# Attention scores on TensorE: fp32 products on 64 partitions each, or split fp32r operands stacked on 128 partitions and always 256 columns wide

## The reference

```python
def neighbourhood_attention(q, k, v, rpb):
    b, t, h, dh = q.shape
    rows = t // GRID_W
    kh = min(NA_KH, rows)
    qg = q.reshape(b, rows, GRID_W, h, dh) * (dh ** -0.5)
    ...
    def one_row(r):
        ...
        s = jnp.einsum('bqhd,bjkhd->bhqjk', qr, kb).astype(jnp.float32)
        ...
        s = jnp.where(col_in[:, None, :], s + bias[None], -jnp.inf)
        p = jax.nn.softmax(s.reshape(b, h, GRID_W, kh * GRID_W), axis=-1)
        p = p.reshape(b, h, GRID_W, kh, GRID_W).astype(vb.dtype)
        return jnp.einsum('bhqjk,bjkhd->bqhd', p, vb)
```

## Time and profile before

| | |
|---|---|
| runs | 2142.4, 2145.27, 2147.19 us (median 2145.27) |
| span of the profiled execution | 2143.2 us |
| own device time of the profiled execution | not listed apart; the median of the runs is 2.1 us above its span |
| PE matmuls busy | 2099.4 us, 98% of the span, at full granted clock |
| DVE, ACT, POOL busy | 51%, 37%, 43% |
| DMA | 86 GB/s in the mean |
| layer 1's 16 steps | from about 1373 us of the span, with the output tail to 2143 us |

### The profile page before, as it was taken

How to read it: one execution, slowest core, us unless ns; L and a number is a source line. 1 busy time by engine, 2 the same in 40 slices (tenths; PEclk the granted TensorE clock), 3 DMA queues, 4 the chain that set the end, 5 groups by cost and what they waited for, 6 DMA issues and landing times.

```text
span 2143.2 us, 31195 instructions
## 1 busy us (share of the span) xinstructions
PE 2099.4 (98%) x12580; PEld 1789.7 (84%) x12580; DVE 1089.1 (51%) x1866; ACT 800.1 (37%) x1943; POOL 924.6 (43%) x623
## 2 busy tenths in 40 slices
PE   8999999999999999999999999999999999999997
PEld 7888887788898888787788887888888888888885
DVE  4104332598898898897712233144333423541447
ACT  4123122465464555473322111143424323432343
POOL 5533332333343343325742332654454445544544
PEclk9999999999999999999999999999999999999999
DMA  5221112335232233235331111322131223123213
GB/s 189 90 68 53 51 50 74 137 98 143 80 109 80 70 118 100 78 119 173 125 125 50 50 50 50 96 87 68 59 88 59 68 59 96 40 68 86 69 50 118
DMA packets 206685, 184.19 MB, mean 86 GB/s; under 512 B 23916, under 2 KB 172684, under 8 KB 206541
## 3 DMA queue, kind: packets, MB, share of 16 engines
q1 hardware_dynamic: 206541, 182.20, 27.7%
HBM read 168.19 MB, written 12.21 MB: 84 GB/s over the span
## 4 chain that ended last, share of the span: by engine, by line
PE 50%; DVE 4%; issue 1%; ACT 0%; DMA 0%; POOL 0%; DVEq 0%; POOLq 0%; ACTq 0%
PE bank L214 25%; PE bank L264 9%; PE bank L574 6%; PE bank L2411 2%; PE bank L2439 2%; PE bank L1067 2%; PE bank L2422 2%; PE bank L1093 1%; DVE acc L944 1%; PE bank L1131 1%; DVE acc L940 1%; DMA R<-macc_dram 0%; PE bank L447 0%; DVE R L422 0%; PE bank L2483 0%
## 5 line engine op out<-in xcount | busy, mean ns | idle before, releaser
L188 POOL TENSOR_SCALAR Wh<-Wraw 128x1024 fp32r<-128x1024 f32 x217 | 245.9, 1133 | 1100.2 <-issue 755.2
L214 PE MATMUL bank<-Hh,Wh 128*128 128x512 f32 (+1 forms) x1936 | 664.6, 343 | 3.2 <-ACT R L817 1.4
L214 PE MATMUL bank<-Hl,Wh 128*128 128x512 f32 (+1 forms) x1936 | 652.0, 337 | 0.0
L214 PE MATMUL bank<-Hh,Wl 128*128 128x512 f32 (+1 forms) x1936 | 651.0, 336 | 0.0
L191 POOL TENSOR_TENSOR Wl<-Wraw,Wh 128x1024 fp32r<-128x1024 f32 x217 | 550.6, 2537 | 18.1
L214 PEld LDWEIGHTS bank<-Hh,Wh 128*128 128x128 f32 x1936 | 367.7, 190 | 51.0 <-issue 10.8
L214 PEld LDWEIGHTS bank<-Hh,Wl 128*128 128x128 f32 x1936 | 367.3, 190 | 39.0
L214 PEld LDWEIGHTS bank<-Hl,Wh 128*128 128x128 f32 x1936 | 367.9, 190 | 36.6 <-issue 1.7
L298 DVE TENSOR_TENSOR acc<-bank,acc 128x512 f32<-128x512 f32 x240 | 165.0, 690 | 166.3 <-PE bank L264 165.5
L264 PE MATMUL bank<-Wh,Mh 128*128 128x512 f32 x528 | 208.7, 395 | 8.7 <-DVE acc L298 7.6
L264 PE MATMUL bank<-Wh,Ml 128*128 128x512 f32 x528 | 205.7, 390 | 0.0
(11 more groups left out here) (259 smaller groups left out, 3124.0 us busy)
## 6 DMA issues: line engine op xcount, KB each, us to landing
Wraw<-in_na_w_in_dram SPq DMA_DIRECT2D x80, 512.0 KB, 3.8
Wraw<-in_ssd_w_in_dram SPq DMA_DIRECT2D x57, 512.0 KB, 4.2
Wraw<-in_w_out_dram SPq DMA_DIRECT2D x48, 512.0 KB, 3.3
R<-acs_dram SPq DMA_DIRECT2D x16, 1536.0 KB, 6.8
Wraw<-in_w_mem_kv_dram SPq DMA_DIRECT2D x32, 512.0 KB, 3.9
R<-gs_dram SPq DMA_DIRECT2D x32, 128.0 KB, 3.5
R<-R SPq DMA_DIRECT2D x32, 128.0 KB, 3.6
macc_dram<-acc SPq DMA_DIRECT2D x1, 3072.0 KB, 11.5
```

The source lines that it names most:

```text
L188: pool.tensor_scalar(Wh[:, s, :], Wraw[:, s, :], 1.0, 1.0, ALU.mult, ALU.mult).then_inc(pool_c, 1)
L214: mm = pe.matmul(DB[h.k % 2][:, 0:t1 - t0], w[:, k, :], x[:, k, t0:t1], start=(k == 0 and i == 0), stop=(k == KC - 1 and i == 2))
```

## The change

The scores are no longer plain fp32 matmuls. The change makes three stacked tensors for each pair of heads, and does two fp32r matmuls over all 128 partitions where there was one fp32 matmul over 64:

- `Qs` (Q_split): for head h, its own 64 rows hold the high part of q, the other 64 rows hold its low part.
- `Kh` (K_high): for head h, the high part of k on both halves of the partitions.
- `Kl` (K_low, and for head 1 M_last_low): the low part of k on the head's own rows, zero on the others.
- `Qs` times `Kh` gives high x high + low x high; `Qs` times `Kl` gives high x low. Both are added in PSUM.
- Every block is computed 256 columns wide, at column 0 or 256 of its bank (`wide`); DVE reads the same 256, 192 or 160 columns as before, and the second blocks of banks 1 and 2 have moved to columns 320 and 256.
- ACT writes the high parts (`split_q`, `split_k`, two copies of 64 x 768 each) and the second copy of the high part of k (`repeat_k`, two more). DVE makes the low parts (`low_parts`, four subtractions of 64 x 768, and once two fills with zeros).
- PE waits for `k_twice` and `qk_low` before the scores.
- `Q_split` and `K_high` lie where `gain` and a part of the residual were kept, so SP loads those two behind the last scores instead of in step 1.

```diff
@@ class Places
                 self.mix = tensor_at("M_last", 0, [P, 3, T], F32R)
+                self.q_split = tensor_at("Q_split", 12096, [P, 2, T], F32R)
+                self.k_high = tensor_at("K_high", 13632, [P, 2, T], F32R)
+                self.k_low = tensor_at("K_low", 10224, [P, T], F32R)
@@ attention_phase
+            Qs, Kh, Kl = place.q_split, place.k_high, [place.k_low[:, :], place.mix_low[:, :]]
+            ROWS_OF = [slice(0, 64), slice(64, P)]
             B = [(0, 0, 256, NP_ + 128, NP_ + 64, 0, 3), (0, 256, 256, NP_ + 256, NP_ + 192, 0, 4),
-                 (1, 0, 192, NP_, NP_, 256, 2), (1, 192, 192, NP_ + 384, NP_ + 320, 448, 5),
-                 (2, 0, 160, 0, 0, 640, 0), (2, 160, 160, 128, 96, 800, 1)]
+                 (1, 0, 192, NP_, NP_, 256, 2), (1, 320, 192, NP_ + 384, NP_ + 320, 448, 5),
+                 (2, 0, 160, 0, 0, 640, 0), (2, 256, 160, 128, 96, 800, 1)]
+            def wide(c0, k0):
+                c = c0 // 256 * 256
+                return slice(c, c + 256), slice(k0 - (c0 - c), k0 - (c0 - c) + 256)
@@ sync
-                    if n == 1:
-                        sp.wait_ge(begun.mixed, 12)
-                        sp.wait_ge(begun.x1_stored, 16)
-                        sp.dma_start(gain, post_g[1:2, :].broadcast_to([P, D])).then_inc(gain_landed, 16)
-                        load_res(sp, 2)
...
                 def end():
                     load_out(sp, 1, slice(14 * P, 16 * P))
+                    sp.wait_ge(begun.x1_stored, 16)
+                    sp.wait_ge(scored, 2 * PAIRS)
+                    sp.dma_start(gain, post_g[1:2, :].broadcast_to([P, D])).then_inc(gain_landed, 16)
+                    load_res(sp, 2)
@@ scalar
+                def split_q(n):
+                    act.wait_ge(dense_free, HF["act"].value + 2)
+                    for h, f in enumerate(ROWS_OF):
+                        i = act.activation(Qs[f, h, :], qF[f, :], ACT.Copy)
+                    i.then_inc(qk_high, 1)
+                def split_k(n):
+                    act.wait_ge(dense_free, HF["act"].value + 2)
+                    for h, f in enumerate(ROWS_OF):
+                        i = act.activation(Kh[f, h, :], kF[f, :], ACT.Copy)
+                    i.then_inc(qk_high, 1)
+                def repeat_k(n):
+                    for h, f in enumerate(ROWS_OF):
+                        i = act.activation(Kh[ROWS_OF[1 - h], h, :], kF[f, :], ACT.Copy)
+                    i.then_inc(k_twice, 1)
@@ scalar, step
                         probs(n - 1, 1)
+                    split_q(n)
                     if n == LAST:
                         act_take(act, [lambda b: act.activation(kF[:, 0:NP_], b[:, 0:NP_], ACT.Copy),
                                        lambda b: act.activation(kF[:, NP_:T], b[:, 0:NS], ACT.Copy)],
                                  between=lambda: take_pt(n - 1, (0,)))
+                        split_k(n)
+                        repeat_k(n)
                         take_pt(n - 1, (1,))
                     else:
                         take_spans(act, kF)
+                        split_k(n)
                         if out_after(n):
                             out_units()
                         if prev:
                             take_pt(n - 1)
+                        repeat_k(n)
@@ vector
+                def low_parts(n):
+                    if n == 0:
+                        for h in range(2):
+                            c.add(dve.memset(Kl[h][ROWS_OF[1 - h], :].bitcast(F32), 0.0))
+                    dve.wait_ge(qk_high, 2 * n + 1)
+                    for h, f in enumerate(ROWS_OF):
+                        dve.tensor_tensor(Qs[ROWS_OF[1 - h], h, :], qF[f, :], Qs[f, h, :].bitcast(F32), ALU.subtract)
+                    dve.wait_ge(qk_high, 2 * n + 2)
+                    for h, f in enumerate(ROWS_OF):
+                        i = dve.tensor_tensor(Kl[h][f, :], kF[f, :], Kh[f, h, :].bitcast(F32), ALU.subtract)
+                    i.then_inc(qk_low, 1)
                 def step(n, a, prev):
+                    low_parts(n)
@@ tensor, score
+                    pe.wait_ge(k_twice, n + 1)
+                    pe.wait_ge(qk_low, n + 1)
...
+                        at, of = wide(c0, k0)
                         for h in range(2):
-                            f = slice(64 * h, 64 * h + 64)
-                            mm = pe.matmul(A[3 * h + bk][:, c0:c0 + w], qF[f, q0:q0 + P], kF[f, k0:k0 + w],
-                                           start=True, stop=True)
+                            pe.matmul(A[3 * h + bk][:, at], Qs[:, h, q0:q0 + P], Kh[:, h, of],
+                                      start=True, stop=False)
+                            mm = pe.matmul(A[3 * h + bk][:, at], Qs[:, h, q0:q0 + P], Kl[h][:, of],
+                                           start=False, stop=True)
```

More of the change, by code:

```diff
@@ L2041, in attention_phase @@
             gain_landed, prompt_gated = sem("n_gain_landed"), sem("n_prompt_gated")
+            qk_high, k_twice, qk_low = (sem("n_" + x) for x in ("qk_high", "k_twice", "qk_low"))
             bias_landed = [sem("n_bias_landed0"), sem("n_bias_landed1")]
```

## The result

The changed kernel took 2149.17 us in the median of 12 executions (2148.53 to 2152.42), the kernel before 2145.68 us (2142.4 to 2148.66, 12 executions). The ratio is 1.0021, 95% interval 1.0013 to 1.0029, which is 4.5 us more (2.8 to 6.2) of 2145.68; the two medians by themselves lie 3.5 us apart. The forecast was 2150.3 us, a ratio of 1.0023 to the median that it started from.

The account below looks back on a forecast made before the run. PE, busy 98% of the span, was taken as the bound, except at the softmax path in the last step. Terms 1.3 + 1.6 + 2.1 = 5.0 us, added to the median, gave 2150.3 us (+0.23%), range 2145.5 to 2153.5.

Parts of the forecast that it names:

- Middle steps: Scores on PE in 11 middle steps: +0.11 us each, 1.3 us in all, bounds 0 to 2.4 us.
- Steps 0, 4, 8, 12: Scores without apply_v right before them and nothing to wait for: +0.41 us, four times, 1.6 us; upper bound 2.4 us.
- the padding of 160 and 192 columns: Score blocks of 160 and 192 columns paid as 256, a third more columns, given as reason for +0.41 us.
- ACT and DVE hidden: Added ACT copies hidden behind PE's z unit with about 1 us spare; DVE's subtractions, 3.8 us a step, cost zero.
- Gain: SP's later load of gain lands about 4.2 us after issue, hidden with 7 us of cover before ACT reads it.
- The last step: Step 15: apply_v(14) waits 2.0 us for take_pt behind four ACT copies, scores end 0.1 us later; +2.1 us.
- the three terms: Middle steps 1.3 us, steps 0, 4, 8, 12 1.6 us, last step 2.1 us: 5.0 us more.
- rival 2: The wait in step 15 is absent or much shorter through quicker copies: +2.9 to 4 us, about 2148.5 us; chance 0.18.
- The faster stream (1): New score matmuls come closer together than 0.119 us; at 0.109, +1.2 us, 2146.5 us; chance 0.15.
- The upper bound of 2.5 us for the last step: Step 15 if copies don't overlap at all (4 x 0.88): a wait of 2.4 us; 2.5 us in rival 3's sum.
- More waits (3): ACT's spare microsecond in middle steps is missing, or waits and shape changes cost upper bounds: 7.3 us, 2152.6 us; chance 0.15.
- The much cheaper scores (4): Scores get much cheaper because half of the passes go; PE would save over 0.5 us a step; chance 0.04.

Follow-up runs that it names:

- g1: Kernel before, with apply_v doing the two prompt blocks first under their own semaphore so DVE gates the prompt earlier; 2138.73 us, ratio 0.9977.
- g3: e1's kernel with apply_v doing the two prompt blocks first and DVE gating the prompt earlier; 2150.26 us in one execution.
- e3: Changed kernel with each score block computed at its own width (256, 192 or 160 columns) instead of always 256; 2149.86 us, ratio 1.0019.
- e5: Kernel before with the score loops swapped: all six blocks of head 0, then all six of head 1; 2162.44 us in one execution.
- e4: Changed kernel with all its copies, subtractions, waits and moved loads, but the scores again as fp32 matmuls on 64 partitions; 2147.93 us in one execution.
- e1: Changed kernel with the four copies of step 15 (split_k, repeat_k) moved behind take_pt; 2147.12 us, ratio 1.0011 to before.
- f8: The changed kernel run once more as it is, to see what of its profile repeats; 2149.22 us.
- f7: e1's kernel with the low product on each head's own 64 partitions, blocks in four groups; 2161.17 us, ratio 1.0071 to before.
- f6: e1's kernel with the low product on each head's own 64 partitions, block by block; 2173.26 us, ratio 1.0131 to before.
- f2: Changed kernel with only repeat_k of step 15 moved behind take_pt, split_k staying in front; 3004.66 us.

## Why the prediction was right

**Middle steps: right in size and in its reason.** 0.10 us a step for 0.11 (11 of them are 1.2 us, and not the 1.3 of the sum). The stream runs at 0.118 us (0.119 forecast), the first interval behind `apply_v` is the slow one (0.224 us for 0.223) and the change to L214 isn't. g1 and g3 confirm that the loss of 0.54 us is set off by 0.44 of vanished waits.

**Steps 0, 4, 8, 12: right.** 0.37 and 0.38 us for 0.41. That these cost more than the middle ones is because nothing waited there before. The reason in the text, the padding of 160 and 192 columns, is refuted by e3: full width costs 0.1 us of it. The columns grow by 26% there (1536 against 1216), not by a third. With own widths the scores still take 2.73 us there, where the old ones take 2.26, and that is the lost sharing (e5): 24 starts one after the other instead of 12 pairs.

**ACT and DVE hidden: right.** ACT's timeline in step 4, beside the earlier trace rows:

```profile
1539.99 0.38 ACT L245 ACTIVATE R<-bank 128x256 f32<-128x256 f32 x1
1540.94 0.60 ACT L246 ACTIVATE R<-bank 128x512 f32<-128x512 f32 x1 [0.56 <-PE bank L214]
```

The cover is 0.56 us where 1 was forecast, and e4 shows that it is enough: 32.90 us with all the copies. DVE is hidden too, but its price was too low: it is busy for 100 us more, 6.2 us a step where the sum had 3.8. The subtractions of 64 x 768 in step 4, and beside them what POOL does meanwhile:

```profile
1532.78 2.72 DVE L2375 TENSOR_TENSOR K_low<-R,K_high 64x768 fp32r<-64x768 f32 x1 [0.36 <-ACT K_high L2226]
1535.51 0.95 DVE L2375 TENSOR_TENSOR M_last_low<-R,K_high 64x768 fp32r<-64x768 f32 x1
```

```profile
1531.70 2.98 POOL L191 TENSOR_TENSOR Wl<-Wraw,Wh 128x1024 fp32r<-128x1024 f32 x1
```

The first one runs against POOL's splitting of a weight unit for 1.90 us and takes 2.72, the second, of the same shape, has POOL idle and takes 0.95. It is so for all of them in the traces of after and of e1: none that had POOL idle took over 0.96 us. In step 15 the low part of k is ready at 2079.56 for it, where the sum had 2078.8, still ahead of `apply_v`.

**Gain: right.** SP issues it at 2097.45 and ACT reads it at 2108.84; it lands in about 4.2 us.

**The last step: the mechanism right, the term too small.** The wait is 2.15 us for 2.0. The step that was off is "copies back to back start about 0.1 us before the previous one ends". ACT's timeline in step 15:

```profile
2074.08 0.60 ACT L2251 ACTIVATE R<-bank 128x512 f32<-128x512 f32 x1 [2.23 <-PE bank L214]
2074.71 1.70 ACT L2226 ACTIVATE K_high<-R 64x768 fp32r<-64x768 f32 x2
2076.44 1.70 ACT L2231 ACTIVATE K_high<-R 64x768 fp32r<-64x768 f32 x2
2078.05 0.57 ACT L2211 ACTIVATE R<-bank 128x512 f32<-128x512 f32 x1
```

Two copies take 1.70 us, 0.85 each without overlap, and from the first of the four to `take_pt` it is 3.34 us where the sum had 3.1. With 0.1 for the scores and about 0.1 around them, f8 has 2.34 us for the 2.1 of the sum; its wait lies inside the bounds given (1.3 to 2.4 us). The 0.88 us a copy of the upper bound is in no row. In that form the three terms are 1.1 + 1.5 + 2.3 = 4.9 us for 5.0, and the ratio's interval holds it.

**How much the number proves.** Little by itself. The forecast of 2150.3 us lies 1.1 us above the measured median, and rival 2's 2148.5, with a short wait or none, lies 0.7 us below it. That the total came out so near is in part luck; it is the terms, read one by one in the traces, that speak for the mechanism.

**What the sum did not have** is the granted clock. In the first profiled execution of after, half clock behind the wait added 1.5 us to it. It isn't a fixed price of the change: of the four traces with the wait of 2.15 to 2.2 us, two have it (after, e3) and two haven't (e4, f8), and without the wait (e1) `apply_v` takes 2.84 us as in before. That the 12 executions of after fall into one group at 2148.5 to 2149.3 and one at 2151.0 to 2152.4 would fit a clock stretch that comes in some of them, but only the profiled execution of each kernel has a trace, so this stays open.

**Rivals.** The faster stream (1) fell: 0.118 us, and with fewer columns it stops at 0.112. The short wait (2) fell with 2.15 us. More waits (3) fell in the middle steps. The much cheaper scores (4) fell. The upper bound of 2.5 us for the last step was passed by the first profiled execution of after (3.87), by the clock alone.

## What to carry to other kernels

Two matmuls on separate halves of the partitions share the array, and a form on all 128 partitions with fewer passes must beat the shared price (here 2.26 us), not the single one (4.1). Here matmuls of 192 and of 160 columns, each with a weight load of 128 columns, cost the same, and those of 256 hardly more, so count matmuls there and not columns. Look for the waits that an added stream would swallow, and remove them first: they made this change look cheap, and taken out by themselves they were worth about what it cost (4.9 us against 4.5). Compare two traces by distances around the same instructions and look up the granted clock in the stretch, because a few microseconds at half clock hide behind the digits of the page.

## What the runs showed of the hardware

- Half clock (1.2 GHz) for some 3 us in single executions of an unchanged program: behind a wait of PE of 2.15 us (after, e3), of 2.44 us in layer 0 (e4, e5, f7, f8, g3) or of 1.9 to 2.0 us in the output tail (e3, f6, g3, with 1.5 us of loss each). It did not follow the same waits in others: the first not in e4 and f8, the second not in before, after, e1, e3 and f6. Once it came inside a stream of matmuls without idle time and lasted some 7 us (before, 266 to 273 us).
- A change between matmuls on 128 and on 64 rows: 0.18 to 0.19 us each (f6, f7), against 0.118 us for a whole matmul of 256 columns.
- fp32r matmuls of 160, 192 and 256 columns: 0.112, 0.112, 0.118 us apart (e3, after). Twelve matmuls of one column took 1.40 us (before).
- A DVE subtraction of 64 x 768 takes 0.95 us with POOL idle and up to 3.06 us while POOL splits weights (after).
- PE starts records of the next matmul on the other half of the partitions while those of the present head still run (0.006 to 0.05 us apart, e5).
- ACT's copies of 64 x 768 take as long as the 843 ns of 128 x 768 in the earlier trace rows, and don't overlap.
- Two executions of this one-core program (one of e1, and f2) took 3004.9 and 3004.7 us, both at a mean granted clock of 0.652. One execution of before, among the 15 beside g1, took 8027.49 us at full clock; it has no trace, and its cause is open.
